# Stick-breaking attention inside one transformer layer: value products in two halves, and the first turned group of every tile copied by VectorE

## What is computed

```python
z = einsum("bhqd,bhkd->bhqk", q_blk, k_pre) * scale
log_rest = where(strict, log_sigmoid(-z), 0.0)
suffix = cumsum(log_rest, axis=3, reverse=True) - log_rest
a = where(strict, exp(log_sigmoid(z) + suffix), 0.0)
out = einsum("bhqk,bhkd->bhqd", a, v_pre)
```

## Time and profile before

| | us |
|---|---|
| median of three runs | 2084.97 |
| lowest and highest of them | 2082.77, 2085.02 |
| the profiled execution's own time | 2086.72 |
| its span in the trace | 2084.9 |
| mean granted clock of TensorE, share of full speed | 0.981 |

### The profile page before, as it was taken

How to read it: one execution, slowest core, us unless ns; L and a number is a source line. 1 busy time by engine, 2 the same in 40 slices (tenths; PEclk the granted TensorE clock), 3 DMA queues, 4 the chain that set the end, 5 groups by cost and what they waited for, 6 DMA issues and landing times. The chain is left out here.

```text
span 2084.9 us, 25157 instructions
## 1 busy us (share of the span) xinstructions
PE 1995.5 (96%) x9345; PEld 1641.0 (79%) x9345; DVE 1332.8 (64%) x1813; ACT 863.2 (41%) x1523; POOL 575.6 (28%) x424
## 2 busy tenths in 40 slices
PE   7999999999999999888799999999999999999997
PEld 5788888887887688666578888887788888878886
DVE  6765565569798532566545565557755655669896
ACT  6434433434445211566534344443443333334443
POOL 1354555430002121154321100121544554510000
PEclk8999999999999999998899999999999999999999
DMA  4223222254300231623034422231232222265102
GB/s 142 81 71 91 81 80 83 86 210 160 130 21 2 85 101 61 162 61 81 6 107 132 131 82 61 61 111 31 81 91 87 78 81 84 76 238 176 61 1 81
DMA packets 216466, 190.15 MB, mean 91 GB/s; under 512 B 7532, under 2 KB 171928, under 8 KB 216344
## 3 DMA queue, kind: packets, MB, share of 16 engines
q1 hardware_dynamic: 216256, 188.51, 29.4%
q10 hardware_dynamic: 88, 0.02, 0.0%
HBM read 152.85 MB, written 35.65 MB: 90 GB/s over the span
## 5 line engine op out<-in xcount | busy, mean ns | idle before, releaser
L1816 DVE TENSOR_TENSOR w_lo<-st,w_hi 128x512 fp32r<-128x512 f32 x160 | 173.4, 1085 | 178.4 <-ACT w_hi L1395 178.3
L946 PE MATMUL ps<-T_hi,w_lo 128*128 128x512 f32 x640 | 249.1, 389 | 0.4 <-issue 0.4
L947 PE MATMUL ps<-T_lo,w_hi 128*128 128x512 f32 x640 | 249.0, 389 | 0.0
L948 PE MATMUL ps<-T_hi,w_hi 128*128 128x512 f32 x640 | 249.0, 389 | 0.0
L946 PE MATMUL ps<-tr_hi,sr_lo 128*128 128x512 f32 x616 | 242.6, 394 | 5.1 <-DVE xT L2047 2.7
L948 PE MATMUL ps<-tr_hi,sr_hi 128*128 128x512 f32 x616 | 240.5, 390 | 0.0
L947 PE MATMUL ps<-tr_lo,sr_hi 128*128 128x512 f32 x616 | 240.4, 390 | 0.0
L946 PE MATMUL ps<-B_hi,w_lo 128*128 128x512 f32 x576 | 226.5, 393 | 9.9 <-DVE w_lo L1816 4.0
L947 PE MATMUL ps<-B_lo,w_hi 128*128 128x512 f32 x576 | 225.3, 391 | 0.0
L948 PE MATMUL ps<-B_hi,w_hi 128*128 128x512 f32 x576 | 225.3, 391 | 0.0
L946 PE MATMUL ps<-act_hi,wb_lo 128*128 128x512 f32 x384 | 153.2, 399 | 3.1 <-DVE wb_lo L1816 1.6
(11 more groups left out here) (257 smaller groups left out, 4250.3 us busy)
## 6 DMA issues: line engine op xcount, KB each, us to landing
gate_raw<-in_ffn_w_gate SPq DMA_DIRECT2D x44, 512.0 KB, 5.2
up_raw<-in_ffn_w_up SPq DMA_DIRECT2D x44, 512.0 KB, 5.1
h_spill<-up_s SPq DMA_DIRECT2D x66, 256.0 KB, 2.0
piece_A<-in_ffn_w_down SPq DMA_DIRECT2D x32, 512.0 KB, 4.5
piece_B<-h_spill SPq DMA_DIRECT2D x32, 512.0 KB, 6.0
wa_raw<-in_w_in SPq DMA_DIRECT2D x16, 512.0 KB, 4.0
wb_raw<-in_w_out SPq DMA_DIRECT2D x16, 512.0 KB, 4.0
wb_raw<-in_mem_w_kv SPq DMA_DIRECT2D x16, 512.0 KB, 3.8
```

Source lines behind the costliest of these rows:

```text
L946: pe.matmul(to, w_lo, m_hi, start=first, stop=False, skip_group_check=joins)
L947: pe.matmul(to, w_hi, m_lo, start=False, stop=False, skip_group_check=joins)
L948: return pe.matmul(to, w_hi, m_hi, start=False, stop=last, skip_group_check=joins)
L1816: return dve.tensor_tensor(to, value, plain(hi), ALU.subtract)
```

## The change

1. `by_dve` returns true for the first turned group of every tile, so the copies of the 32 short tiles go from ACT to DVE. ACT keeps the second turned groups of the long tiles. The semaphore counts that PE waits for in `turned`, `values` and behind the loop are changed to fit.
2. `values(w)` is cut in two: the first half of its products at step 4w + 9, the second half at step 4w + 10. The waits stand ahead of the first half; `s_o` is incremented behind the second.
3. `OUT_LAG` goes from 10 to 11: ACT's rounding of group w is at step 4w + 11. DVE's remainder is one step behind that, at 4w + 12.

```diff
         def by_dve(m, first):
-            return tile_at(m)[1] >= 4 and first == 0
+            return first == 0

         def turned(nth):
             m, first = turn_of[nth]
-            return (s_aT_dve, long_tiles(m)) if by_dve(m, first) else (s_aT, m + 1)
+            return (s_aT_dve, m + 1) if by_dve(m, first) else (s_aT, long_tiles(m))

-        STICK_LAG, TURN_LAG, VALUE_LAG, OUT_LAG = 1, 4, 9, 10
+        STICK_LAG, TURN_LAG, VALUE_LAG, OUT_LAG = 1, 4, 9, 11

-            def values(w):
+            def values(w, part):
                 hp, b = group_at(w)
-                pe.wait_ge(s_aT, 4 * w + 4)
-                if b >= 2:
-                    pe.wait_ge(s_aT_dve, long_tiles(4 * w + 3))
-                if w:
-                    pe.wait_ge(s_o_free, w)
+                if part == 0:
+                    pe.wait_ge(s_aT_dve, 4 * w + 4)
+                    if b >= 2:
+                        pe.wait_ge(s_aT, long_tiles(4 * w + 3))
+                    if w:
+                        pe.wait_ge(s_o_free, w)
                 n = 2 * b + 2
-                for j in range(n):
+                for j in range(part * n // 2, (part + 1) * n // 2):
...
-                mm.then_inc(s_o, 1)
+                if part:
+                    mm.then_inc(s_o, 1)

-                if VALUE_LAG <= s < M + VALUE_LAG and (s - VALUE_LAG) % 4 == 0:
-                    values((s - VALUE_LAG) // 4)
+                if VALUE_LAG <= s < M + VALUE_LAG and (s - VALUE_LAG) % 4 < 2:
+                    values(*divmod(s - VALUE_LAG, 4))

-            pe.wait_ge(s_aT, M)
-            pe.wait_ge(s_aT_dve, long_tiles(M - 1))
+            pe.wait_ge(s_aT_dve, M)
+            pe.wait_ge(s_aT, long_tiles(M - 1))

# DVE's loop
-                if s >= OUT_LAG and (s - OUT_LAG) % 4 == 0:
-                    w = (s - OUT_LAG) // 4
+                if s > OUT_LAG and (s - OUT_LAG - 1) % 4 == 0:
+                    w = (s - OUT_LAG - 1) // 4
```

## The result

The median of four runs is 2068.65 us (2066.05 to 2069.16), against 2084.95 in four runs of the kernel before: 16.3 us less, a ratio of 0.9922 with a 95% interval of 0.9905 to 0.9939. In a later comparison the same kernel gave 0.9916 [0.9900, 0.9932]. The profiled execution of the kernel after is the lowest of its four, 2066.05; the one of before took 2086.72, 1.8 above its median. So the two traces differ by 20.7 us where the medians differ by 16.3.

The account below looks back on a forecast made before the run. In-order queues waiting for each other bound the attention stage, DVE nearest to a bound. Gains of 1.6 (pair 0), 8.0 (pairs 1 and 2), 3.5 (pair 3) and 1.2 (tail) sum to 14.3 us: 2071.5 us, range 2062 to 2080.

Parts of the forecast that it names:

- Stretches A and B: DVE's wide scans with 128/256-tile copies, then wide-tile copies: 9.2 and 6.1 us, gains 1.5 and 0.6.
- Stretch C: DVE's third stretch of a head pair, taking the 384/512-tile copies: 10.35 us including 0.6 for PE's late turn, gain 1.4.
- rival 2: Half the gain: gaps move to other waits, A and C give 0.8 each, about 6 us, 2080; chance 0.15.
- Stretch D: Fourth stretch of a head pair, bound by PE's work: gain 0.5 us, with the clock as it was.
- Rival 1: Shorter waits keep TensorE's clock at 2.4 GHz in D and the tail: 9 us more, 2062.5; chance 0.17.
- The tail: End of the attention stage: halved products hold a turn back less, last values wait 0.4 us; gain 1.2 us.
- Behind the stage: After the attention stage PE runs dense, so nothing there takes the gain back.
- The copies: Eight copies per head pair moved to DVE: 0.30 to 0.68 us each by record, 3.3 us per pair after overlap.
- The new wait: First half of values(w) waits for s_o_free from a later remainder: priced at nothing, uncovered about 0.4 us in A and C.
- The signs of being wrong: DVE gap over 1.5 us in A or C, PE's 1.60 us copy wait growing, or PE awaiting the remainder.
- Rival 3: DVE becomes the bound in C and A: 3.3 us a pair slower, 13 us, 2100; chance 0.07.
- Rival 4: No change worth the name, since PE's order and the scans alone set the stage: 2085; chance 0.06.

Follow-up runs that it names:

- same-step kernel: The kernel after with DVE's remainder in the step of ACT's rounding (4w + 11), no longer one behind: 2080.77 us, ratio 0.9981 to the kernel before.
- halves and lag: The kernel after with the copies of the short tiles back on ACT: 2062.16 us, ratio 0.9888 to the kernel before.
- filled kernel: The kernel before with 12 useless score products in each of two PE idle gaps ahead of D, head pairs 1 to 3: 2085.56 us, ratio 0.9996.
- copies only: The kernel before with only the short-tile copies moved to DVE, whole values and old steps: 2091.72 us, ratio 1.0031.
- copies and halves: The kernel after with rounding and remainder back at step 4w + 10: 2075.97 us, ratio 0.9962 to the kernel before.
- copies and lag: The kernel after with whole values instead of two halves: 2072.12 us, ratio 0.9944 to the kernel before.
- second profile: The unchanged kernel after, run and profiled again beside a later set: 2067.88 us, ratio 0.9916 to the kernel before.
- best ends: The kernel after without moved copies, two weight tiles loaded before SP's wait and weight splits put behind the last copy: 2059.78 us, ratio 0.9881.
- Halves only: The kernel before with value products in two halves, rounding and remainder at step 4w + 10, old copies: 2071.07 us, ratio 0.9934.
- both filled kernels: Useless products in PE's idle time: the kernel before, ahead of D (2085.56 us), and best ends, at the end of A (2058.20 us).

## Why the prediction was right, and where not

It named 2071.5, 2062 to 2080, faster with 0.82; it is 2068.65. The order of the work did what was told in A and B. That the sum came so near is partly luck, as the terms show.

*Stretches A and B.* 9.2 and 6.1 predicted, 9.06 and 6.11 measured. The mechanism as told is shown: with the remainder two steps down and the values halved, A runs without a gap on DVE. The same-step kernel puts 1.3 us back into A, 0.86 of it a wait for `act_hi`.

*Stretch C.* 10.35 predicted, 10.80 measured. The term for PE's late turn was mis-sized, 0.6 for the 1.07 us that DVE waits at 935.45. PE is busy 9.92 of 10.80, and halves and lag, where DVE has 1.9 us less to do in C, is only 0.26 shorter there. So C is set by PE's side of the chain now, as rival 2 said of it, and not by DVE's work plus one late turn; that 9.76 + 0.6 came near is partly luck.

*Stretch D.* The largest error in a pair: 0.5 taken, 1.90 measured. "With the clock as it was" failed: D ran at 1.00. By the filled kernel 1.63 of it is the clock; the order alone gave less than I took, 0.27. Rival 1 had that the clock comes with it, and its price for D (1.7), right. Its condition, shorter waits of PE, holds in sum, but not where it looked. The wait of 1.60 us on DVE's copy ahead of D did not get shorter; what went is the one for ACT's copy that stood just ahead of it. The first line is of before, the second of after:

```profile
942.15 0.33 PE L1248 MATMUL ps<-ident,beta 128*128 128x128 f32 x1 [1.45 <-ACT aT L1395]
...
938.53 0.85 PE L1248 MATMUL ps<-ident,beta_last 128*128 128x128 f32 x6 [1.66 <-DVE aT L2246]
```

Ahead of D PE waited 3.05 us before and 1.66 after. The profiles of all the kernels that fill nothing there bear this out, with D of pairs 0 to 2 in each. With 3.0 to 3.3 us of such waits (before, copies only) D is below 1.00 in six of six; with 2.2 to 2.8 (copies and halves, copies and lag, same step) in four of nine; with 1.5 to 1.8 (the other eight profiles) in two of 24. So the kernel after won the clock in D by shorter waits, and less idle time makes the fall rarer but does not rule it out. The rival was also not the whole truth, since B is still at 0.78 to 0.63 in some pairs. At full clock throughout, a pair before takes 10.72 + 6.72 + 11.74 + 7.90 = 37.1 us, after 33.6, so that 3.5 of my 4.0 us a pair are from the order. In the two traces the pairs 0 to 3 and the tail gained 3.0, 5.1, 6.9, 3.3 and 5.2 us, 23.4 in all, where I had 1.6, 4.0, 4.0, 3.5 and 1.2, 14.3 in all. The sum came near the medians' 16.3 because no term for the clock, somewhat high ones for the order, 2.3 us given back behind the stage (and 0.3 ahead of it) and a gap of 4.4 between traces and medians met.

*The tail.* 1.2 taken, 5.2 in the first trace. The last 12 products took 2.60 us for 4.96 and the 8 before them 1.95 for 3.26: 3.7 us of clock, which the second profile shows in part only (13.87 for 11.15). That leaves at most 1.5 for the order, close to the 1.2.

*Behind the stage.* "Nothing there takes the gain back" was wrong for this profile: 2.3 us, and 1.2 in the second one. Halves and lag gave nothing back (1043.75), and best ends won 2.

*The copies.* Their cost on DVE was right: 0.278, 0.398, 0.530 and 0.682 us against 0.30, 0.425, 0.555 and 0.68. The estimate from the Trainium skill, VectorE: DVE Perf Modes, section on the TRN2 errata, was 0.26, 0.39, 0.53 and 0.66, so for copies this short its cycle count holds as well as my line. Their effect on the stretches was not: I had 0.91 in A and 2.15 in C, and taking them away gives 0.22 and 0.26 (halves and lag), since another wait fills most of the place. That they are a loss in themselves was in the sum but not said, and the best version is the change without them. I had written that what ACT is relieved of "alone gives nothing", and this is what the copies-only kernel shows, down to a loss.

*The new wait.* Priced at nothing: in pairs 0 to 3 PE does not wait for the remainder ahead of the values. It does once, at the end:

```profile
1014.01 0.41 DVE L1819 TENSOR_TENSOR act_lo<-ps,act_hi 128x256 fp32r<-128x256 f32 x1
...
1014.57 2.60 PE L1267 MATMUL ps<-aT,v_all 128*64 128x256 f32 x24 [3.12 <-DVE act_lo L1819]
```

The 3.12 us are not the price of the new wait. PE stood 3.02 us ahead of the same products before, behind the same two weight splits and the last copy; the remainder adds its own 0.41, the 0.4 that the tail had. Best ends, where the splits come later, brings this wait to 1.3.

*The signs of being wrong.* DVE's longest gap in A or C is 1.07 us, under 1.5. PE's wait of 1.60 us for DVE's copy is 1.66, so by the letter it grew; and PE waits for the remainder, once. Neither kept D or the tail from getting shorter.

*What I read wrongly in the profile.* I took the 30.0 us in front of `act_lo` as the thing to be won. Halves only keeps 25.3 of them and gains 14.7 us. The wait was one sign of a chain with three links: values, scores and sigmoid, remainder. Loosening it in either of the two places that were tried gave most of the gain, and at C's 10.5 us PE took over.

*The rivals.* Rival 2's own sum, 0.8 in A of three pairs and in C of four, less 0.9, is 4.7 and not 6. Rival 3 (DVE becomes the bound, slower) is true of A, where DVE is busy 9.06 of 9.06, but from a lower level; the copies-only kernel at +6 us is what it described, where nothing else is loosened. Rival 4 is out.

## What to carry to other kernels

When engines are held by in-order queues, put an instruction that waits for another engine behind work whose input is ready, even a step or two later; here this gave 19.6 us by itself, a part of it through the clock. Do not add work to the engine nearest to its bound because another looks loaded: test each part of a change alone, since here the best result is the change less one of its parts. And where TensorE idles between short bursts, a time is made of two things, the order and the clock; compare stretches at the same granted clock before you credit either.

## What was not expected of the hardware

The granted clock of a stretch is not a property of the kernel alone. The same B took 6.11 us at 1.00 and 7.66 to 8.68 at 0.78 to 0.63, in different pairs of one execution and between two executions of one kernel (the pair 0 of after). It hangs on the idle time of PE ahead of it: D was below 1.00 in six of six places behind waits of 3.0 to 3.3 us and in two of 24 behind 1.5 to 1.8, and filling such time put the stretch behind it at 1.00 in all seven places that were filled, five of which were below that in the profile without filling. But it is not fixed by it: the same waits of 1.19 and 0.68 us left B at 1.00 in one pair and at 0.78 in the next, and in both filled kernels another stretch was low. The Trainium skill, TensorE: Matmul & The Clock Gate, Part 1, says that the moment of a change also varies from run to run; the trace agrees, with the pair 0 and the last stretch of after. A single profile can be off by a few us in such a stage, here 3.8 between two of one kernel.
